# Turning the first step's rows inside the one-hot product, with the last tile's shift added on GpSimd

## The reference, cut to what matters

```python
for l in range(DEPTH):                                # DEPTH = 2
    ...                                               # modulation, mixer, xp/xs = x + ga1 * out
    hp = rms_norm(xp, norm2_g[l]) * (1.0 + sc2p) + sh2p
    hs = rms_norm(xs, norm2_g[l]) * (1.0 + sc2s) + sh2s
    xp = xp + ga2p * hier_moe(hp, ...)
    xs = xs + ga2s * hier_moe(hs, ...)

def hier_moe(h, wg, bg, we, be, w1, w3, w2):
    ...                                               # gates: two experts per token
    hid = silu(einsum('bld,edf->blef', h, w1)) * einsum('bld,edf->blef', h, w3)
    return einsum('blef,efd->bld', hid * gates[..., None], w2)
```

## Time and profile before

| | us |
|---|---|
| median of 3 runs | 755.17 |
| lowest and highest run | 753.98, 755.49 |
| span of the profiled execution, first to last instruction | 748.4 |
| difference between that span and the median | 6.8 |
| TensorE busy | 685.6 (92% of the span) |
| VectorE busy | 246.5 (33%) |
| ScalarE busy | 142.0 (19%) |
| GpSimd busy | 165.4 (22%) |

### The profile page before, as it was taken

The page is one execution under the profiler, slowest core; times in us unless marked ns, Lnnn a source line. Parts: engine busy times, 40 slices in busy tenths (PEclk is TensorE's granted clock), DMA queues, the critical chain, the costliest instruction groups (busy, mean ns, idle before and its releaser), DMA issues.

```text
span 748.4 us, 9564 instructions
## 1 busy us (share of the span) xinstructions
PE 685.6 (92%) x3667; PEld 387.9 (52%) x3667; DVE 246.5 (33%) x525; ACT 142.0 (19%) x291; POOL 165.4 (22%) x221
## 2 busy tenths in 40 slices
PE   1799999999999999899989999899899999999990
PEld 0344444564565666556444454356445566666650
DVE  0200312211237223223551423555312733232346
ACT  2100100000221212112132110555112122121201
POOL 5000111011331122212111100357223122222202
PEclk9899999999989999999999999999999899999996
DMA  9999999299539999998580685904501969989842
GB/s 336 394 363 345 381 410 388 82 404 424 244 143 394 407 423 421 420 422 351 198 324 2 249 332 186 376 2 184 183 1 41 409 269 417 421 358 421 332 174 100
DMA packets 53207, 219.46 MB, mean 293 GB/s; under 512 B 13773, under 2 KB 20941, under 8 KB 33968
## 3 DMA queue, kind: packets, MB, share of 16 engines
q1 hardware_dynamic: 31520, 178.59, 59.7%
q0 software_dynamic: 9664, 23.41, 8.3%
q10 hardware_dynamic: 11984, 16.92, 6.5%
HBM read 206.53 MB, written 20.68 MB: 304 GB/s over the span
## 4 chain that ended last, share of the span: by engine, by line
PE 73%; DMA 16%; DVE 6%; issue 2%; ACT 2%; POOL 0%; SPq 0%; ACTq 0%; POOLq 0%; DVEq 0%
PE ps L1396 13%; PE ps L1310 11%; PE ps L1468 7%; PE ps L1421 6%; DMA pool<-in_mod_w 5%; PE ps L1504 5%; PE ps L1245 4%; DMA pool<-in_moe_w 4%; DMA pool<-h_rows,of_now 4%; PE ps L1455 3%; PE ps L1485 3%; PE ps L1638 3%; PE ps L1563 2%; PE ps L1298 2%; PE ps L1383 2%
## 5 line engine op out<-in xcount | busy, mean ns | idle before, releaser
L1396 PE MATMUL ps<-pool 128*64 128x256 f32 x928 | 103.6, 379 | 2.2 <-issue 2.1
L1396 PEld LDWEIGHTS ps<-pool 128*64 128x64 f32 x928 | 76.5, 137 | 31.5 <-issue 9.5
L1310 PE MATMUL ps<-pool,turned 128*128 128x512 f32 x192 | 84.6, 595 | 0.0
L1245 PE MATMUL ps<-pool,cs 128*32 128x512 f32 x384 | 48.3, 630 | 18.5 <-DMA pool<-in_mod_w 9.7
L1468 PE MATMUL ps<-turned,pool 128*128 128x384 f32 x192 | 65.1, 492 | 0.0
L1310 PEld LDWEIGHTS ps<-pool,turned 128*128 128x128 f32 x192 | 35.7, 190 | 41.3 <-issue 41.1
L1421 PE MATMUL ps<-pool 128*64 128x512 f32 x240 | 54.8, 597 | 1.9 <-DMA pool<-in_moe_w 0.8
L1468 PEld LDWEIGHTS ps<-turned,pool 128*128 128x128 f32 x192 | 36.8, 196 | 30.9 <-issue 8.9
L964 DVE SCALAR_TENSOR_TENSOR pool<-ps,pool 128x256 f32<-128x256 f32 x20 | 9.7, 484 | 113.0 <-PE ps L1396 113.0
L417 POOL TENSOR_SCALAR rstd<-ss 128x1 f32<-128x1 f32 x24 | 10.6, 441 | 160.1 <-ACT xn L583 119.6
L547 POOL TENSOR_SCALAR pool<-pool 128x384 f32<-128x384 f32 (+1 forms) x30 | 30.5, 1031 | 59.3 <-DVE pool L1159 59.2
(11 more groups left out here) (245 smaller groups left out, 899.7 us busy)
## 6 DMA issues: line engine op xcount, KB each, us to landing
pool<-in_moe_w SPq DMA_DIRECT2D x72, 1024.0 KB, 15.1
pool<-in_mod_w SPq DMA_DIRECT2D x24, 2048.0 KB, 12.6
turned<-in_moe_w SPq DMA_DIRECT2D x18, 1024.0 KB, 14.4
pool<-in_ev_w_in SPq DMA_DIRECT2D x6, 1024.0 KB, 20.0
y_rows<-pool ACTq DMA_DIRECT2D x8, 768.0 KB, 20.2
xn<-in_moe_w SPq DMA_DIRECT2D x6, 1024.0 KB
pool<-y_rows ACTq DMA_DIRECT2D x12, 512.0 KB, 6.6
pool<-in_ev_w_in SPq DMA_DIRECT2D x2, 2048.0 KB, 23.1
```

Of the source, the lines that this page charges most:

```text
L1245: ins = mm(ps[32 * j:32 * j + 32, 7, :], cs32[:, 2 * part + c, :], w[:, c, j * 512:(j + 1) * 512], start=part + c == 0, stop=part + c == 4)
L1310: ins = mm(ps[:, 2 * t + n, :], yT[:, k, t * P:(t + 1) * P], weight(parts[k // 4], 4, D)[:, k % 4, n * 512:n * 512 + 512], start=k == 0, s ...
L1396: ins = mm(ps[m, k, 0:DE], hTe.rearrange("p (c n) -> p c n", c=DC)[:, cc, m], w[e][:, cc, :], start=cc == 0, stop=cc == DC - 1)
```

## The change

`first_rows` makes the rows of the first step turned: the rows `xn` are now the stationary operand, a chunk of the width at a time, and `first_hot` moves, 128 columns. 24 products (8 chunks, 3 tiles each) write banks 2 and 3 directly. The copies to `ys`, the eight transposes and the `keep_clock` product of 384 columns are gone. `first_mm` now tells that bank 2 is full, and `L0_x_tr` takes its place in the wait of the last place of weights. The shift of tile 2 moves from VectorE to GpSimd, directly behind VectorE's scaling, and all products wait for it (`h_last`).

```diff
@@ expert_places @@
-  ... (("first_mm", 2), ("L1_gathered", 16))[l] ...
+  ... (("L0_x_tr", 1), ("L1_gathered", 16))[l] ...
@@ GpSimd, rows_made @@
                     if t == TILES - 1:
-                        gps.wait_ge(S("h_last"), l + 1)
+                        gps.wait_ge(S("last_scaled"), l + 1)
+                        ch.link(nc.gpsimd.tensor_tensor(xn[:, t, :], xn[:, t, :], hrow[:, 1, cond_of(t), :], ALU.add))
+                        gps.sem_inc(S("h_last"), 1)
                         gps.dma_start(h_rows[t * P:(t + 1) * P, :], xn[:, t, :]).then_inc(S("h_rows"), 16)
@@ ScalarE, experts @@
-                act.wait_ge(S("first_mm"), 2 * l + 1)
-                a_.activation(ys[:, 0:512], ps[:, 6, :], ACT.Copy).then_inc(S("first_act"), 1)
-                turned_tokens(0)
+                act.wait_ge(S("first_mm"), l + 1)
+                a_.activation(hTe[:, 0:512], ps[:, 2, :], ACT.Copy).then_inc(S(f"L{l}_hTe"), 1)
@@ VectorE, router @@
-                link(v_.scalar_tensor_tensor(xn[:, t, :], x[:, t, :], rstd[:, t:t + 1], hrow[:, 0, cond_of(t), :], ALU.mult, ALU.mult))
+                v_.scalar_tensor_tensor(xn[:, t, :], x[:, t, :], rstd[:, t:t + 1], hrow[:, 0, cond_of(t), :], ALU.mult, ALU.mult) \
+                    .then_inc(S("last_scaled"), 1)
@@ VectorE, place_tokens @@
-                t = TILES - 1
-                v_.tensor_tensor(xn[:, t, :], xn[:, t, :], hrow[:, 1, cond_of(t), :], ALU.add).then_inc(S("h_last"), 1)
@@ VectorE, experts @@
-                dve.wait_ge(S("first_mm"), 2 * l + 2)
-                v_.tensor_copy(ys[:, 512:], ps[:, 7, :]).then_inc(S("first_dve"), 1)
                 step_contents(l)
@@ TensorE, first_rows @@
-                for half in range(2):
+                pe.wait_ge(S("h_last"), l + 1)
+                for cc in range(DC):
                     for t in range(TILES):
-                        if (half, t) == (0, TILES - 1):
-                            pe.wait_ge(S("h_last"), l + 1)
-                        ins = mm(ps[:, 6 + half, :], first_hot[:, t, :], xn[:, t, half * 512:(half + 1) * 512],
+                        ins = mm(bank2(2, D)[:, cc * P:(cc + 1) * P], xn[:, t, cc::DC], first_hot[:, t, :],
                                  start=t == 0, stop=t == TILES - 1)
-                    ins.then_inc(S("first_mm"), 1)
+                    if cc == DC // 2 - 1:
+                        ins.then_inc(S("first_mm"), 1)
+                ins.then_inc(S(f"L{l}_x_tr"), 1)
@@ TensorE, experts @@
                 first_rows(l)
-                keep_clock(1, 384)
-                pe.wait_ge(S("first_act"), l + 1)
-                pe.wait_ge(S("first_dve"), l + 1)
-                turn_rows(range(DC), ys)
                 step_contents(l)
```

More of the change, by code:

```diff
@@ L234, in expert_places @@
                 used = {}
-                for o in (owner[s], owner[s + 1]) if s < NSLOT else ((("router_mm", 3 * (l + 1)), ("h_rows", 16 * TILES * (l + 1)), (("first_mm", 2), ("L1_gathered", 16))[l])[0:s - NSLOT + 1]):
+                for o in (owner[s], owner[s + 1]) if s < NSLOT else ((("router_mm", 3 * (l + 1)), ("h_rows", 16 * TILES * (l + 1)), (("L0_x_tr", 1), ("L1_gathered", 16))[l])[0:s - NSLOT + 1]):
                     used[o[:-1]] = max(used.get(o[:-1], 0), o[-1])
@@ L1378, in experts, with turn_rows @@
                 halves = [slice(e * HALF, (e + 1) * HALF) for e in range(2)]
-                def turn_rows(chunks, rows=hg):
+                def turn_rows(chunks):
                     for cc in chunks:
-                        ins = tr(bank2(2, D)[:, cc * P:(cc + 1) * P], rows[:, cc::DC], ident)
+                        ins = tr(bank2(2, D)[:, cc * P:(cc + 1) * P], hg[:, cc::DC], ident)
                         if cc == DC - 1:
```

## The result

The changed kernel has a median of 760.57 us (6 runs, 759.6 to 764.5) where the kernel before had 754.0 on the same chip (6 runs): ratio 1.0104 over all runs, 95% interval 1.0075 to 1.0134 (the two medians alone give 1.0087). The forecast was 752.7, within 751.2 to 755.2. It was wrong in sign and outside its range. The profiled execution took 760.4, its span is 758.5: 1.9 lie around the span. The span is 10.1 longer than that of before, the median only 6.6. In every run whose span is known the time was 1.75 to 1.98 above the span, so the execution profiled before (span 748.4) took some 750.3: 4.9 under the median of its first three runs and 3.7 under that of all six.

A forecast was written before the change was run, and what follows sets the result against it. Layer 0 was taken as bound by the weight stream, layer 1 by VectorE's chain to the first step. Gains of 1.7 us (layer 1) and 0.8 (layer 0), 2.5 together, took 755.17 to 752.7, range 751.2 to 755.2.

The forecast's parts named there:

- Part 2: TensorE's turned one-hot product: 48 passes at 0.112 us, 5.4 in all, ending before VectorE; upper end 0.128 a pass.
- rival (e): One-hot product: short passes lose the clock or don't flow, 0.223 us each; slower, 758.6; chance 7%.
- Part 1: VectorE's chain before the first step loses the addition L893 and copy L976, ending 1.9 us earlier at 234.77.
- Part 3: Shift addition on GpSimd: covered by 5.8 us, but costs VectorE between nothing and 0.4 us; 0.2 taken.
- rival (c): VectorE stands still beside GpSimd's addition for the whole overlap: 0.2 us less gain, 752.9; chance 18%.
- Part 5: Layer 0's weight stream: last place issued near 234.7, closing the gap at 237 to 240; gain 0.8 us.
- Part 4: Layer 1: first step, gather and weight loads behind it all start 1.7 us earlier; gain 1.7.
- The step from span to median: Whole kernel: 6.8 us around the span don't change, so span 745.9 becomes median 752.7.

The follow-up runs named there:

- e13: Changed kernel with product and turns loading every fourth column and the first two weight matrices in 4 KB pieces; ratio 1.0093 to the kernel before.
- e15: e13 with the addition on VectorE right behind its scaling and two more filler products in each layer; ratio 1.0067 to the kernel before.
- e16: Changed kernel with contiguous product weights (result differs), the addition on VectorE behind its scaling, two more fillers a layer; ratio 0.9945 to the kernel before.
- e1: Changed kernel with the one-hot product's weights from 128 neighbouring columns, not every eighth (result differs); 749.35 us, ratio 0.9958 to the kernel before.
- e12: Kernel before with the first two weight matrices of every expert in 1 KB pieces and turns taking contiguous columns; ratio 1.0131.
- e4: Kernel before with only the last tile's shift addition moved to GpSimd, behind VectorE's scaling; ratio 1.0041.
- e6: Kernel before with VectorE's shift addition moved right behind its own scaling of the last tile; ratio 1.001.
- e2: Kernel before with the router's 48 transposes as real float32 products of the same operands; single run 770.18 us.
- e14: Changed kernel with product and turns loading every second column and the first two weight matrices in 2 KB pieces; 754.65 us, ratio 1.0004 to the kernel before.

## Why the prediction was wrong, point by point

**Part 2 failed.** "the transposes load such columns too, at 0.89 / 8 = 0.11, so I keep 0.112": this step priced the pass wrongly. The address pattern was the same and the operation wasn't: a transpose doesn't pay for the step, a real float32 product does, 0.244 for 0.112 a pass, so the product took 11.72 us and not 5.4. By the forecast's own rate (0.48 us a layer for each 0.01 above 0.119) that is 6 us; measured were 5.6 (L1371 at 240.39, not 234.8). The upper end of 0.128 came from a row with contiguous weights and bounded nothing: the one thing new in the pass, its address pattern, had no row, and I took the nearest row by address and not by operation. The kernel's own rows held a warning. L1255 takes 64 weights from every eighth column in real products:

```profile
L1255 PEld LDWEIGHTS ps<-cst,mrow x32: 195/217/217, 32.0 to 33.8; 128*64 128x64 f32 x32
```

64 contiguous columns load in 137 ns elsewhere in that kernel (L1396, also at clock 1.00). By that ratio my estimate of a pass would have been 0.112 x 217 / 137 = 0.177, beyond the 0.160 from which rival (e) decides.

**Rival (e)** was nearest in time (758.6, given 7%) and had the right place, but its mechanism is not what happened: the passes take 0.24 at the full clock too. The lower clock is real and smaller, 1.0 to 1.6 us of the product in a layer where the loads are cheap, and nothing where the step already hides it (11.44 in e13, partly at 0.50, and in e15, at 1.00). Its guess that layer 0 would absorb the delay failed too: the idle 1.83 is gone, but TensorE still waits 1.05 for weights at 329.30 (before 0.83 at 324.86), since they are late as well.

**Part 1 held in its size, and its exact end was luck.** VectorE's chain ended at 234.72 for a forecast 234.77, but it began 0.9 earlier than before (L838 at 221.89, L837 at 222.79), since TensorE gave it the last logits sooner. From there it took 12.83 for 13.92: 1.94 less for the two instructions, 1.15 more for the block, and 0.3 less than these give. The 0.3 come from a wait that the kernel before had:

```profile
228.15 0.16 DVE L887 SCALAR_TENSOR_TENSOR pool<-ps,pool 128x6 f32<-128x6 f32 x1 [0.46 <-PE ps L1339]
```

Its counterpart in the changed kernel starts without a wait, so up to there the block cost 0.7 and not 1.15 (6.08 us for 5.36). The chain behind the one-hot matrix was not on the path in the changed kernel. e16, where it is, shows the first step 1.8 earlier.

**Part 3 was too small.** I bounded the price at 0.4 because I thought only of the overlap behind 222.79. L838 came earlier (221.89), fell well inside the addition and stood still until its end: 1.15 and 0.88 us more than 0.17. That is the mechanism of rival (c), with a higher price than its 0.4. The one-hot product waits for this part of VectorE's chain, so the block was on the path. The rule of the Trainium skill (SBUF — State Buffer, "Who interferes with whom") has this mechanism, and the trace of after agrees with it in both layers: L838 ends with the addition, and the reductions L861 and L862, with one input, start under it and take 0.17 and 0.19 as before.

**Part 5** assumed that the product ends at the same time. It ended 6.1 later than forecast (240.55, not 234.45), and the gap grew from 1.2 us' worth of bytes to three microseconds. Behind it the first gather landed late (the next turn of rows waits 2.82 for it, before 0.74), and the loads of results start at 367.03, 4.6 later than 362.44. Part 5 had no term for that gather. From issue to landing it took 6.49 us before, 8.24 in the changed kernel and 7.94 in e16; why it takes longer was not tested.

**Part 4**: layer 1 lost 3.6 (12.90 for 9.33) where 1.7 was to be gained. The sum of the trace: 4.6 in layer 0, some 2.8 up to layer 1's product (598.38 for 590.94), 3.6 there, 0.9 given back behind layer 1's first step: 10.1. Of the 2.8, 1.4 is one product L1498 that took 7.90 us where its like took 6.46; the profiled execution had its clock at the lower level for part of that stretch:

```profile
380.00:390.00 10.00, 8.29 (x24) 4.27 (x23) 6.34 (x9) 3.70 (x8) 2.49 (x4) 0.83 0.69 272
```

Most of the rest is the product L1605 at 536.35, 2.78 us for 1.48 (clock 0.66 from 535 to 540, before 1.00). e16's profile has the same fall at the first of these places (7.90), e1's has not (6.46). What brings such falls in one execution and not in another was not settled, nor whether these 2.7 us belong to the change; the medians differ by 3.5 less than the spans.

**The step from span to median was wrong too.** "Around the span lie 6.8 us that don't change": 1.9 lie there, and 4.9 were the distance of that execution from the median. It did no harm to the difference of 2.5, but it hid that the rows of before came from a favourable execution. Where it was faster isn't known. That its product ran at clock 1.00 is not special by itself: it did in e12 too (5.39, 5.39). But e4, e6 and e2 have the same product partly at a lower clock (7.01, 6.85, 7.67, 7.46). The forecast's terms were made to tenths of a microsecond from an execution 5 us off its median.

## What to carry to other kernels

Price a new instruction by a row of the same operation with the same address pattern, and if no row has both, put the two nearest rows at the two ends of the bound; a transpose is no witness for a product. Before making a tile the stationary operand of a float32 product, look at the distance of its columns: 8 bytes cost 5% of the product here (5.89 us for 5.60), 16 doubled it (11.44). Before counting an instruction that is removed, look at what the next one waits for: the addition alone was worth nothing (e6). When an edit takes a wait away, ask who else waits for the instruction that now ends last: here the weight stream did, and turned one late product into a hole in another resource.

## What the runs showed of the hardware

A weight load of 128 float32 columns took 192, 197, 330 and 336 ns with columns 1, 2, 4 and 8 apart in real products, at the full clock (medians; changed kernel, e1, e13, e14). At 8 apart a load took 338 at clock 0.50 and 336 at 1.00, and the pass of 0.24 us was the same; contiguous columns took 333 at 0.50 (e1). Transposes of columns 8 apart loaded in 191. Elementwise engines reading 8 apart took 2.14 for 1.14 (ScalarE), 2.13 for 1.28 (VectorE) and 2.85 for 2.34 (GpSimd, one of two inputs). A two-operand VectorE instruction that starts under one on GpSimd ended with it (1.32 and 1.05 us for 0.17), and reductions with one input did not. Weight transfers in pieces of 8, 4, 2 and 1 KB moved 421, 414, 403 and 379 GB/s.
